# Where VectorE forms the modulation sums in the feed-forward of a three-layer fp32 block chain

## Chip, cores and metric

One core of one Trainium2 chip (trn2) runs the whole program in one launch. The metric is the device time of the launch in microseconds (us); lower is better. All data are fp32 in HBM.

## What is computed

The reference applies two layers of a diffusion-like block (each modulated by vectors made from `c` and `c_ctx`) and then a third block to 256 tokens, beside which run 256 context tokens. Cut to what matters here:

```
mod = silu(c) @ ada_w[l] + ada_b[l]          # six parts of 1024: sh1, sc1, g1, sh2, sc2, g2
h = h + g1 * mixer(rms_norm(h, norm1_g) * (1 + sc1) + sh1)
h = h + g2 * ((silu(a @ w1) * (a @ w3)) @ w2)   with a = rms_norm(h, norm2_g) * (1 + sc2) + sh2
```

The feed-forward of the first layer works on 512 tokens (latent and context), with `w1` and `w3` of 1024 x 2816 and `w2` of 2816 x 1024. While it runs, the kernel also makes the rest of the modulation: `g2` of layer 0 and all six parts of layer 1. `silu(c) @ ada_w` is a product of one or two vectors with a large matrix.

## The kernel before

**Weights.** fp32 products are made on TensorE from two parts of each number. A weight tile of up to 1 MB (128 x 2048) is loaded by SyncE's queue (SP) into `raw` of a slot of SBUF; ScalarE copies it rounded to `whi` (line 1339), VectorE subtracts to get `wlo` over `raw` (line 1840), and TensorE then does three products per block of 128 rows (`mm3`, lines 860 to 862). A slot is free again when the tile's last product is done.

**Modulation sums.** Parts 5 to 11 of the list `MODS` are not made on TensorE. For each there are four tiles of `ada_w`, transposed on the host, of 128 x 2048, and VectorE multiplies each half of such a tile with a row of `silu(c)` or `silu(c_ctx)` and adds up along the row (`summed`, line 1873: a `scalar_tensor_tensor` with `accum_out`). A tile takes four such instructions where both vectors are wanted, two where only one is; at the fourth tile of a part a small `tensor_tensor` adds the bias (line 1893). A sum's tile lies in a slot as a weight tile does, and frees it when its last product is done.

**The order of tiles.** TensorE's program, in a first pass without a chip, lays down the list `TILES`: in the feed-forward, one sum's tile behind each weight tile (`consumed`, line 839, takes the next of `SUMS[12:]`), 28 in all. The document calls the 36 weight tiles of this stage W0 to W35, and the sum's tiles S0 to S27; S0 lies between W0 and W1, S27 between W27 and W28. Tiles take the least recently used of four slots, so as long as the two kinds alternate, the weight tiles go back and forth between the slots named 140/139 and 69/68 (`wlo`/`raw`), and the sum's tiles between 63/60 and 67/64.

The stage has two blocks. Block 1 is W0 to W17, block 2 is W18 to W35. Each has twelve tiles of `w1` and `w3` in turn (`ff1`, `ff3`; two features of 128 per tile, the last two tiles of a block one feature and half the size) and then six of `w2` (`ff2`, two halves of three tiles; the third is of three quarters the size). S0 to S11 take four products each, S12 to S27 two. After W11 a small transpose and a copy hand out the gate row (`gate_rows(5)`).

**Who loads in which order.** SP loads tiles in the order of `loaded()` (line 573): the weight tile first and the sum's tile before it in `TILES` second, so W1, S0, W2, S1 and so on. Each load waits until the slot's previous tile is done, and all later loads wait behind it.

**Who prepares when.** ScalarE and VectorE call `feed(event)` ahead of each step. It goes through the tiles that are new within two tiles of the product named by the event (`next_tiles`, line 583). ScalarE makes the high parts and skips sum's tiles. VectorE's `feed` (line 1831) puts a sum's tile on the list `owed` when it meets it, and makes the low part of a weight tile. Owed sums are formed in two places: before a low part whose own or an earlier load needs the slot that a sum still holds (`held_by`), and at the end of `feed`, if the sum's tile lies before the event's tile. `add(n)` does up to n instructions of the oldest owed sum; `at["sums"]` is 0 up to the end of the first attention (there the sums are spread over its steps) and 4 from there on, set at line 2236.

In the steady state of the feed-forward the order on VectorE is thus: low part of W2, sum S0, activation work of the pair (lines 2264 and 1907: `silu(w1 part) * w3 part`, two features, and their low parts), low part of W3, sum S1, low part of W4, sum S2, activation work, and so on. Each step of TensorE on two features takes one weight tile.

Of the kernel before, what the change touches and what calls it, by code (L numbers as in the profile page):

```python
# [156 lines left out]
class Book:  # L157
# [5 lines left out]
    def did(self, name, *key, by=1):  # L163
        sem = SEM_OF.get(name, name)
        self.now[sem] += by
        if self.counting:
            assert (name, *key) not in self.at, (name, key)
            assert self.by.setdefault(sem, self.engine) == self.engine, (name, sem)
            self.at[name, *key] = sem, self.now[sem]
        assert self.at[name, *key] == (sem, self.now[sem]), (name, key)  # L170
        return self.sems.get(sem), by
# [105 lines left out]
def _build(nc, ctx, I, cst_d, scr_d, out_d, packed):  # L277
# [295 lines left out]
    def loaded():  # L573

        out, held = [], []
        for i, t in enumerate(TILES):
            held.append(i)
            if not t.sums:
                out += held[-1:] + held[:-1]
                held = []  # L580
        return out

    def next_tiles(at, *events):
        n = max([place[event] for event in events], default=0)
        busy = max([i for i in range(max(n - 4, 0), n) if not TILES[i].sums], default=0)
        while at["tile"] < len(TILES):
            i, t = at["tile"], TILES[at["tile"]]
            if t.gate != at["gate"] or t.slot not in at["slots"] or i >= n + at["ahead"] or (not t.sums and t.prev is not None and t.prev >= min(n - 1, busy)):
                return
            at["tile"] += 1  # L590
            yield i, t
# [1225 lines left out]
    def vector_program(e):  # L1817
        at = dict(tile=0, due=Due(book), gate="", chain=0, ahead=2, sums=0, slots={0, 1, 2, *slot_e}, begun=None, owed=[])

        def due(*events):  # L1820
            return at["due"](*events)
# [8 lines left out]
        def feed(*events):  # L1830
            n = max([place[event] for event in events], default=0)
            for i, t in next_tiles(at, *events):
                if t.sums:
                    at["owed"].append(i)
                    continue
                while at["owed"] and held_by(at["owed"][0]) <= loaded().index(i):
                    add(9)
                for s, m in due(("hi", i)):
                    e.wait_ge(s, m)
                e.tensor_tensor(t.lo(), t.raw(), t.hi().bitcast(F32), ALU.subtract).then_inc(*did("lo", i))  # L1840
            while at["sums"] and at["owed"] and at["owed"][0] < n:
                add(at["sums"])

        def held_by(i):

            return next((loaded().index(j) for j in range(i + 1, len(TILES)) if TILES[j].prev == i), len(TILES))

        def add(n):

            i = at["owed"][0]  # L1850
            if at["begun"] is None:
                at["begun"] = summed(i, TILES[i])
            for _ in range(n):
                if next(at["begun"], None) is None:
                    at["begun"] = None
                    at["owed"].pop(0)
                    return
# [5 lines left out]
        def summed(i, t):  # L1863
            p, jj = t.sums
            gate, nv = MODS[p][3], vectors_of(p)
            for s, n in due((f"raw{t.slot}", i), ("cb",), *gm_free(p)):
                e.wait_ge(s, n)
            for c in range(2):
                for v in range(nv):
                    k = 2 * jj + c  # L1870
                    x = GM_OF[p][:, v * 8 + k:v * 8 + k + 1] if gate else MODT_OF[p][:, 2 * k + v:2 * k + v + 1]
                    junk = slot_sum[t.slot][:, (c * nv + v) % 2 * 1024:(c * nv + v) % 2 * 1024 + 1024]
                    m = e.scalar_tensor_tensor(out=junk, in0=slot_raw[t.slot][:, c * 1024:c * 1024 + 1024], scalar=1.0,  # L1873
                                               in1=CB[:, v * D:(v + 1) * D], op0=ALU.mult, op1=ALU.mult, accum_out=x)
                    if (c, v) == (1, nv - 1):
                        m.then_inc(*did("msum", p, jj))
                    elif v == nv - 1:
                        m.then_inc(*link())
                        for s, n in linked():
                            e.wait_ge(s, n)  # L1880
                    yield True
            if jj < 3:
                return
            l, part = MODS[p][:2]
            bias = VT[:, VROW["ada_b"] + l * 48 + part * 8:VROW["ada_b"] + l * 48 + part * 8 + 8]
            for s, n in due(("msum", p, 3)):
                e.wait_ge(s, n)
            if gate:
                x, b3 = v3(GM_OF[p][:, 0:8 * nv], nv), bias.rearrange("p (o k) -> p o k", o=1).broadcast_to([128, nv, 8])
            else:  # L1890
                x = MODT_OF[p].rearrange("p (k v) -> p k v", v=2)[:, :, 0:nv]
                b3 = bias.rearrange("p (k o) -> p k o", o=1).broadcast_to([128, 8, nv])
            e.tensor_tensor(x, x, b3, ALU.add).then_inc(*did("gsum" if gate else "spr", p))

        def gate_rows(p):
            added(p)
            n_ = 8 * MODS[p][3]
            feed(("gt", p))
            for s, n in due(("gt", p), *([("gw", past_gate(p))] if past_gate(p) else [])):
                e.wait_ge(s, n)  # L1900
            e.tensor_copy(G16[0:n_, :], bank("gt", p)[0:n_, 0:128]).then_inc(*did("gcp", p))
            empties(("gt", p), ("gcp", p))
# [23 lines left out]
        def norm_turned(N, p):  # L1926
            w = NORM[N]
            sc, sh, gains = w["mod"][p]
            for k0 in range(0, KT, 2):
                feed(("nt", N, p, k0))  # L1930
                c = p * 4 + k0 // 2
                if k0 % 4 == 0:
                    for s, n in due(("nt", N, p, k0), *gains, *(tm_free(N, c)), *w["tm_free"]):
                        e.wait_ge(s, n)
                    for k in (k0, k0 + 1):
                        o = slice((k - k0) * 256, (k - k0) * 256 + 256)
                        i_ = bank("nt", N, p, k0)[:, o]
                        if sh is None:
                            m = e.tensor_scalar(w["tm"][c % 3][:, o], i_, sc(k), None, ALU.mult)
                        else:  # L1940
                            m = e.tensor_scalar(w["tm"][c % 3][:, o], i_, sc(k), sh(k), ALU.mult, ALU.add)
                    m.then_inc(*did("ntm_v", N, p, k0))
                    empties(("nt", N, p, k0), ("ntm_v", N, p, k0))
                if k0:
                    norm_lo(N, p, k0 - 2)
            norm_lo(N, p, KT - 2)
# [9 lines left out]
        def row(p, hf):  # L1956
            g = 2 * p + hf
            feed(("mod", p, hf, 1))
            for s, n in due(("mod", p, hf, 1), *row_used(p, hf)):
                e.wait_ge(s, n)  # L1960
            e.tensor_copy(GROW[g % 2][0:4, :], bank("mod", p, hf)[0:4, :]).then_inc(*did("grow", p, hf))
            empties(("mod", p, hf), ("grow", p, hf))
# [980 lines left out]
```

## Time and profile before

| | |
|---|---|
| median of 3 runs | 2064.36 us (2060.88 to 2065.09) |
| the profiled execution | 2061.86 us |
| its span in the trace | 2060.0 us |
| TensorE busy | 1789.2 us, 87% |
| VectorE busy | 1246.3 us, 60% |
| ScalarE busy | 823.7 us, 40% |
| mean of DMA traffic | 161 GB/s |
| feed-forward of layer 0 | about 390 to 776 us of the span |

The profiled execution's own time is 1.9 us above its span, which is what lies around the traced part. Rows of the timeline begin with the start in us from the start of the span and the duration in us; an instruction's idle time before it and what ended it stand in square brackets. TensorE's granted clock is given as a share: 1.00 is 2.4 GHz, 0.50 is 1.2 GHz.

### The profile page before, as it was taken

The numbers are of one execution on the slowest core, as the hardware profiler recorded it, in microseconds if no ns is written. First come the engines' busy times: TensorE is split into PE (matmuls) and PEld (weight loads), VectorE is DVE, ScalarE is ACT, GpSimd is POOL, SyncE is SP. The second block draws the span as 40 slices with busy tenths as digits, with TensorE's granted clock in tenths as the row PEclk, the third lists the DMA queues.
The fourth block names the chain that finished last, engine by engine and source line by source line (L and its number), as shares of the span: only waits on it lengthen the run. The fifth ranks groups of instructions, "written<-read, shape, count | busy, mean of one in ns | idle before, by whom it ended". The sixth has DMA issues, their size and how long they took to land. (4 is left out here: it accounts for less than half of the span.)

```text
span 2060.0 us, 21353 instructions
## 1 busy us (share of the span) xinstructions
PE 1789.2 (87%) x8622; PEld 1485.9 (72%) x8622; DVE 1246.3 (60%) x1716; ACT 823.7 (40%) x996; POOL 116.7 (6%) x116
## 2 busy tenths in 40 slices
PE   4988999699799995859767999999987899878997
PEld 2766777487678884749646888888867866668986
DVE  5455782377545535554636888888875555555643
ACT  5222231422113224222314777677744433525532
POOL 1310001000100011320010000000000000000000
PEclk8897988799999997975676999999998999998999
DMA  6322331255545432210033888888855521125552
GB/s 277 102 102 93 132 125 39 102 189 184 194 158 204 163 113 73 84 67 13 1 137 109 326 324 332 324 325 324 322 197 179 176 93 40 62 94 194 183 194 102
DMA packets 61146, 332.54 MB, mean 161 GB/s; under 512 B 16804, under 2 KB 17379, under 8 KB 27890
## 3 DMA queue, kind: packets, MB, share of 16 engines
q1 hardware_dynamic: 55792, 321.54, 42.8%
q10 hardware_dynamic: 4354, 6.32, 0.9%
q0 software_dynamic: 896, 3.26, 0.4%
q8 instruction: 70, 1.15, 0.2%
q14 instruction: 34, 0.27, 0.0%
HBM read 329.96 MB, written 1.13 MB: 161 GB/s over the span
## 5 line engine op out<-in xcount | busy, mean ns | idle before, releaser
L1840 DVE TENSOR_TENSOR wlo__69<-raw__68,whi__70 128x2048 fp32r<-128x2048 f32 (+3 forms) x64 | 136.1, 2127 | 93.4 <-ACT whi__70 L1339 93.4
L1840 DVE TENSOR_TENSOR wlo__65<-raw__64,whi__66 128x2048 fp32r<-128x2048 f32 (+4 forms) x55 | 123.4, 2244 | 76.3 <-ACT whi__66 L1339 76.3
L1840 DVE TENSOR_TENSOR wlo__61<-raw__60,whi__62 128x2048 fp32r<-128x2048 f32 (+4 forms) x56 | 108.6, 1939 | 86.2 <-ACT whi__62 L1339 86.2
L1339 ACT ACTIVATE whi__70<-raw__68 128x2048 fp32r<-128x2048 f32 (+3 forms) x64 | 114.1, 1783 | 115.1 <-DMA raw__68<-in_ffn_w 47.9
L1339 ACT ACTIVATE whi__66<-raw__64 128x2048 fp32r<-128x2048 f32 (+4 forms) x55 | 100.0, 1818 | 77.0 <-DMA raw__64<-in_ev_w_in 21.6
L1339 ACT ACTIVATE whi__62<-raw__60 128x2048 fp32r<-128x2048 f32 (+4 forms) x56 | 91.2, 1628 | 72.8 <-DMA raw__60<-in_ev_w_in 20.7
L2757 POOL TENSOR_TENSOR keep__58<-keep__58,keep__59 128x1 f32<-128x1 f32 (+3 forms) x48 | 45.4, 948 | 1199.3 <-DVE keep__58 L1912 1199.3
L1339 ACT ACTIVATE whi__141<-raw__139 128x2048 fp32r<-128x2048 f32 (+2 forms) x16 | 28.1, 1754 | 126.9 <-DMA raw__139<-in_ffn_w 126.9
L860 PE MATMUL ps<-ffn__120,wlo__140 128*128 128x512 f32 x176 | 70.3, 399 | 9.8 <-DVE wlo__140 L1840 7.0
L1840 DVE TENSOR_TENSOR wlo__140<-raw__139,whi__141 128x2048 fp32r<-128x2048 f32 (+2 forms) x16 | 33.5, 2092 | 72.5 <-ACT whi__141 L1339 72.4
L2095 DVE TENSOR_REDUCE keep__58<-ps 128x1 f32<-128x256 f32 (+1 forms) x104 | 56.6, 544 | 28.5 <-PE ps L862 21.7
L861 PE MATMUL ps<-ffn__121,whi__141 128*128 128x512 f32 x176 | 70.1, 398 | 0.0
L862 PE MATMUL ps<-ffn__120,whi__141 128*128 128x512 f32 x176 | 69.7, 396 | 0.0
L860 PE MATMUL ps<-ffn__120,wlo__69 128*128 128x512 f32 x168 | 65.6, 391 | 2.1 <-issue 2.1
L862 PE MATMUL ps<-ffn__120,whi__70 128*128 128x512 f32 x168 | 65.4, 389 | 0.0
L861 PE MATMUL ps<-ffn__121,whi__70 128*128 128x512 f32 x168 | 65.3, 389 | 0.0
L1873 DVE SCALAR_TENSOR_TENSOR wsum__71<-raw__68,silu_rows 128x1024 f32<-128x1024 f32 x48 | 56.7, 1219 | 2.9 <-DMA raw__68<-in_ada_w 2.8
L1840 DVE TENSOR_TENSOR wlo__218<-raw__217,whi__219 128x2048 fp32r<-128x2048 f32 x24 | 54.9, 2286 | 4.1 <-ACT whi__219 L1339 4.1
L1840 DVE TENSOR_TENSOR wlo__222<-raw__221,whi__223 128x2048 fp32r<-128x2048 f32 x24 | 54.8, 2284 | 0.0
L1840 DVE TENSOR_TENSOR wlo__226<-raw__225,whi__227 128x2048 fp32r<-128x2048 f32 (+1 forms) x24 | 50.6, 2108 | 3.8 <-ACT whi__227 L1339 3.8
L1339 ACT ACTIVATE whi__219<-raw__217 128x2048 fp32r<-128x2048 f32 x24 | 45.8, 1910 | 6.9 <-DMA raw__217<-in_moe_w 6.9
L1873 DVE SCALAR_TENSOR_TENSOR wsum__63<-raw__60,silu_rows 128x1024 f32<-128x1024 f32 x40 | 48.0, 1222 | 0.5
(1069 smaller groups left out, 5376.7 us busy)
## 6 DMA issues: line engine op xcount, KB each, us to landing
raw__217<-in_moe_w SPq DMA_DIRECT2D x24, 1024.0 KB, 6.6
raw__221<-in_moe_w SPq DMA_DIRECT2D x24, 1024.0 KB, 6.7
raw__225<-in_moe_w SPq DMA_DIRECT2D x16, 1024.0 KB, 5.7
raw__68<-in_moe_w SPq DMA_DIRECT2D x16, 1024.0 KB, 6.3
raw__64<-in_moe_w SPq DMA_DIRECT2D x16, 1024.0 KB, 6.8
raw__60<-in_ada_w SPq DMA_DIRECT2D x15, 1024.0 KB, 5.8
raw__64<-in_ada_w SPq DMA_DIRECT2D x15, 1024.0 KB, 5.7
raw__68<-in_ffn_w SPq DMA_DIRECT2D x14, 1024.0 KB, 4.9
```

The source lines that it names most:

```text
L860: e.matmul(out, ll, rh, start=start, stop=False)
L861: e.matmul(out, lh, rl, start=False, stop=False)
L862: return e.matmul(out, lh, rh, start=False, stop=stop)
L1339: e.activation(t.hi(), t.raw(), ACT.Copy).then_inc(*did("hi", i))
L1840: e.tensor_tensor(t.lo(), t.raw(), t.hi().bitcast(F32), ALU.subtract).then_inc(*did("lo", i))
L1873: m = e.scalar_tensor_tensor(out=junk, in0=slot_raw[t.slot][:, c * 1024:c * 1024 + 1024], scalar=1.0, in1=CB[:, v * D:(v + 1) * D], op0=AL ...
L2095: e.tensor_reduce(neg, b[:, 0:u.total], AX.X, ALU.max).then_inc(*link())
L2757: e.tensor_tensor(x, x, EXPO[:, 0:1].broadcast_to([128, n_]) if n_ > 1 else EXPO[:, 0:1], ALU.pow).then_inc(*did(out, *key))
```

## The change

In VectorE's `feed`, when a sum's tile is met and `at["sums"]` is not 0, the sum is formed on the spot, in full, before the low part of the next weight tile. Nothing else is touched: the tiles, their slots, SP's order of loads, ScalarE's and TensorE's programs stay.

```diff
@@ -1832,6 +1832,8 @@
             for i, t in next_tiles(at, *events):
                 if t.sums:
                     at["owed"].append(i)
+                    while at["sums"] and at["owed"]:
+                        add(at["sums"])
                     continue
                 while at["owed"] and held_by(at["owed"][0]) <= loaded().index(i):
                     add(9)
```

With it VectorE's order in the feed-forward is: low part of W0, sum S0, low part of W1, sum S1, low part of W2, activation work, sum S2, low part of W3, sum S3, low part of W4, activation work, and so on. The number of instructions is the same. Outside the feed-forward no sum's tile is met while `at["sums"]` is not 0.

## Rows read from the trace of the kernel before

**Rows 1.** The page's first part: busy us, share of the span, instructions.

```profile
PE 1789.2 (87%) x8622; PEld 1485.9 (72%) x8622; DVE 1246.3 (60%) x1716; ACT 823.7 (40%) x996; POOL 116.7 (6%) x116
```

**Rows 2.** Busy time by stretch: length, PE, PEld, DVE, ACT, POOL, PEclk, DMA, GB/s.

```profile
425.50:447.30 21.80, 21.80 (x98) 17.88 (x96) 16.29 (x23) 5.96 (x6) 0.00 (x0) 1.00 0.56 194
...
625.00:647.00 22.00, 22.00 (x98) 18.22 (x98) 12.09 (x15) 6.26 (x7) 0.00 (x0) 1.00 0.50 193
```

**Rows 3.** Timeline of PE: first products of weight tiles of the feed-forward.

```profile
425.52 0.39 PE L860 MATMUL ps<-ffn__120,wlo__69 128*128 128x512 f32 x1
...
436.40 0.39 PE L860 MATMUL ps<-ffn__120,wlo__140 128*128 128x512 f32 x1
...
508.12 0.47 PE L860 MATMUL ps<-ffn__120,wlo__69 128*128 128x512 f32 x1 [0.75 <-issue]
...
516.55 0.47 PE L860 MATMUL ps<-whi__141,ffn__128 128*128 128x512 f32 x1 [2.60 <-DVE wlo__140 L1840]
...
530.54 0.47 PE L860 MATMUL ps<-whi__70,ffn__128 128*128 128x512 f32 x1 [2.87 <-DVE wlo__69 L1840]
...
557.98 0.79 PE L860 MATMUL ps<-whi__70,ffn__128 128*128 128x512 f32 x1 [6.48 <-DVE ffn__135 L2146]
...
593.13 0.64 PE L860 MATMUL ps<-ffn__120,wlo__140 128*128 128x512 f32 x1 [2.79 <-issue]
...
607.25 0.47 PE L860 MATMUL ps<-ffn__120,wlo__69 128*128 128x512 f32 x1 [1.37 <-issue]
```

**Rows 4.** Timeline of DVE: one pair of block 1, then the end of a two-product sum.

```profile
432.80 2.29 DVE L1840 TENSOR_TENSOR wlo__140<-raw__139,whi__141 128x2048 fp32r<-128x2048 f32 x1 [2.93 <-ACT whi__141 L1339]
435.00 1.22 DVE L1873 SCALAR_TENSOR_TENSOR wsum__63<-raw__60,silu_rows 128x1024 f32<-128x1024 f32 x1
...
439.71 0.68 DVE L2264 TENSOR_TENSOR ffn__134<-ffn__131,ps 128x512 f32<-128x512 f32 x1
...
443.08 0.69 DVE L1907 TENSOR_TENSOR ffn__128<-ffn__132,ffn__127 128x512 fp32r<-128x512 f32 x1 [0.70 <-ACT ffn__127 L1384]
...
451.92 0.17 DVE L1893 TENSOR_TENSOR keep__54<-keep__54,keep__51 128x16 f32<-128x16 f32 x1
...
554.83 1.22 DVE L1873 SCALAR_TENSOR_TENSOR wsum__67<-raw__64,silu_rows 128x1024 f32<-128x1024 f32 x1
...
557.24 0.69 DVE L2146 TENSOR_TENSOR ffn__135<-ps,keep__57 128x512 f32<-128x512 f32 x1
```

**Rows 5.** Timeline of SP: loads of weight tiles (139, 68) and a sum's tile (64).

```profile
403.95 0.33 SPq L2861 DMA_DIRECT2D raw__139<-in_ffn_w  x1
404.32 0.44 SPq L2861 DMA_DIRECT2D raw__64<-in_ada_w  x1
...
425.71 0.33 SPq L2861 DMA_DIRECT2D raw__139<-in_ffn_w  x1
...
595.84 0.43 SPq L2861 DMA_DIRECT2D raw__68<-in_ffn_w  x1
```

**Rows 6.** Issues to landing (last column, us): sum's tiles issued at 404.32, 618.82, 502.33.

```profile
raw__64<-in_ada_w SPq DMA_DIRECT2D x1, 1024.0 KB, 7.0
...
raw__60<-in_ada_w SPq DMA_DIRECT2D x1, 1024.0 KB, 8.3
...
raw__60<-in_ada_w SPq DMA_DIRECT2D x1, 1024.0 KB, 5.8
```

**Rows 7.** Timeline of ACT: the high part of the tile loaded at 425.71.

```profile
430.85 1.92 ACT L1339 ACTIVATE whi__141<-raw__139 128x2048 fp32r<-128x2048 f32 x1 [8.01 <-DMA raw__139<-in_ffn_w]
```

**Rows 8.** Stretches as in rows 2: the wait before W12, then W13, W15, W18.

```profile
514.00:518.00 4.00, 1.45 (x7) 1.24 (x7) 3.88 (x4) 0.56 (x2) 0.00 (x0) 1.00 0.89 352
530.54:543.18 12.64, 12.63 (x49) 10.24 (x49) 1.76 (x1) 1.48 (x1) 0.56 (x1) 0.86 0.47 183
557.98:571.14 13.16, 13.16 (x48) 10.67 (x49) 4.04 (x4) 1.92 (x1) 4.99 (x4) 0.83 0.47 194
593.13:605.72 12.59, 12.59 (x48) 10.05 (x48) 8.08 (x14) 1.92 (x1) 5.05 (x4) 0.86 0.65 251
```

## Prediction

> **What bounds the kernel now.** I read the page first: TensorE is busy 87% of the span [rows 1]. Then the stretches of the one stage where the change acts, the feed-forward. In a pair of weight tiles of block 1 and in one of block 2 TensorE is busy throughout, at the full clock [rows 2]: it bounds the stage, and any time by which a weight tile comes late is lost. VectorE is busy 16.3 of 21.8 us in block 1 and 12.1 of 22.0 in block 2 [rows 2], so it has room, but only over a pair, not at each point of it. Third, TensorE's timeline: a weight tile lasts 10.9 us (425.52 to 436.40), and the idle stretches stand at W11, W12, W13, W15, W18 and W19 [rows 3]. Fourth, how late a weight tile is made ready: its load leaves 0.2 us after the product before it ends (425.71 for 425.52) [rows 3, 5], ScalarE starts 5.1 us later and takes 1.9 [rows 7], the low part runs 432.80 to 435.09 [rows 4], and TensorE wants it at 436.40 [rows 3]. The margin is 1.3 us. The sum that follows the low part at 435.00 is already beyond that point and costs TensorE nothing.
>
> **The change, part by part.** The same instructions run; 28 sums move from behind a low part to in front of one. Two things then stand between a weight tile's load and its product: the wait for the sum's own tile, and the sum.
>
> Terms, in us. (a) The sum's tile is issued 0.37 behind the weight tile [rows 5]: SP's order is as before, and the sum two back, which holds its slot, is now always done. It landed 7.0 after its issue once and 8.3 after it another time [rows 6], so 7.4 to 8.7 behind the weight tile's issue. I take 7.7, nearer the first, because it is the landing inside this steady stretch; the ends stay for the range. Behind a tile of half the size it is 0.4 + 5.8 = 6.2 [rows 6]; behind three quarters I put 6.8, between the two. (b) Four products take 4.7 (435.00 to 439.71), with the bias 0.2 more; two take 2.4 (554.83 to 557.24) [rows 4]. (c) The low part takes 2.2 to VectorE's next instruction (432.80 to 435.00) and 2.4 to TensorE's start: 2.3 of duration, and 0.05 as from line 2146's end (557.93) to 557.98 [rows 3, 4]. Of half size I put 1.2 and 1.3, half of it. (d) The activation work takes 4.1 (439.71 to 443.77) [rows 4].
>
> *W1* (no cost). S0 is loaded ahead of the stage, W1's low part has a whole tile of TensorE as its cover.
>
> *Block 1, the four even tiles W2, W4, W6, W8.* Counted from the first product of the odd tile before: load at 0.2, sum's tile at 7.9, products to 12.6, low part, TensorE starts at 15.0. It wanted to start at 10.9: **+4.1 each**. *The odd tiles between.* Their load leaves at 11.1, their sum's tile lands at 18.8; VectorE has just finished the activation work (14.8 + 4.1 = 18.9). Products to 23.6, TensorE could start at 26.0 and is busy until 25.9: nothing. Four times 4.1 and 0.2 of bias twice: 16.8.
>
> *The clock.* A wait of 2.60 left the granted clock at 1.00; waits of 2.87 and 2.79 were followed by tiles at a mean of 0.86 that lasted 12.6 instead of 10.9, one of 6.48 by 13.2 at 0.83 [rows 3, 8]. So in these rows the wait of 2.60 kept 2.4 GHz, and those of 2.79 and 2.87 were followed by a while at 1.2 GHz that cost 1.7 us. The new waits of 4.1 are longer than both: 4 x 1.7 = 6.8. The even tile then ends at 27.6, and the odd tile's preparation is hidden outright. The Trainium skill (TensorE: Matmul & The Clock Gate, section Why this matters for your kernels) asks for no idle gap above about 3 us between bursts; by it the waits of 2.87 and 2.79 should have been free, and the trace says they were not. By that rule the four waits of 4.1 still cost the clock, and the sum would be the same.
>
> *The end of block 1.* W10 (half size): 0.2 + 6.2 + 4.7 + 1.3 = 12.4 against 10.9: +1.5. W11: its load leaves 1.3 before W10's start, so it starts 6.2 + 4.7 + 1.3 - 1.3 = 10.9 after it; before, 5.4 + 0.9 (the 0.75 of idling and the tail of a product [rows 3]) = 6.3: +4.6. W12: load 5.6 after W10's start, then 7.7 + 4.9 + 2.4, so 9.7 after W11's start; before 8.4 (508.12 to 516.55) [rows 3]: +1.3. W13 was 14.0 behind W12 (to 530.54) because S11 and the low part queued up on VectorE; now only 2.4 of products stands before it, it waits for TensorE alone, at 10.9 or with a slow clock 12.6, I take 11.5: -2.5. W13 itself ran at 0.86 for 12.6 [rows 8]; W14 follows after 0.2 + 6.8 + 2.4 + 1.8 = 11.2: -1.4. W15 waited for line 2146, which stood behind the low part of W15 and two sums; it began 14.8 after W14 (543.18 to 557.98) [rows 3, 8]. Now: load and sum's tile 7.7, products 2.4, low part 2.2, line 2146 0.7, so 13.1: -1.7. W16, nothing; W17 +0.3. W18: 12.4 behind W17 instead of 11.1 (571.14 + 10.9 = 582.02 to 593.13) [rows 3, 8]: +1.3. W19 began 14.1 after W18; its load had been held by SP behind S17's, which waited for S15, until 595.84 [rows 5]. Now that load leaves when W17 is done, the wait of 1.37 [rows 3] goes, and W19 follows at 12.6: -1.5. Together: +1.5 + 4.6 + 1.3 - 2.5 - 1.4 - 1.7 + 0.3 + 1.3 - 1.5 = +1.9.
>
> *Block 2, W20, W22, W24, W26.* 0.2 + 7.7 + 2.4 + 2.4 = 12.7 against 10.9: +1.8 each and 0.2 of bias twice: 7.6. These waits are shorter than the one of 2.60, so no clock. The odd tiles: sum's tile at 11.1 + 7.7 = 18.8, start possible at 23.6, TensorE busy until 12.7 + 10.9 = 23.6: nothing. From W28 on there are no sums.
>
> *Queues.* On SP no load waits longer for a sum than before. POOL's gate row load after W11 shifts with the stage and has the same room before line 2146. ScalarE waits for activation work that comes later, and its next high part is done well before VectorE ends the next sum. The stages behind start from the last residual of this one, so nothing takes the delay up.
>
> Sum: 16.8 + 6.8 + 1.9 + 7.6 = **33 us**. Against the profiled execution, 2061.86, this gives 2095. The median of the runs shown is 2.5 us higher; I keep 2095, 31 above it.
>
> **Rivals.**
>
> *The clock holds.* If the waits, spread differently against the clock's steps, leave it at 1.00, the 6.8 go: 26, so 2088. For it: the wait of 2.60 did so [rows 3, 8]. Against: 4.1 is well over both waits that did not. 15%.
>
> *Late landings.* If the sum's tile lands at 8.7 every time [rows 6], the four even tiles of block 1, the tiles W10 to W12, W15, W18 and the four of block 2 take 1.0 more, 13 in all; block 2's waits become 2.8, as long as the one that cost the clock, 4 x 1.7 more, less what W13's slack takes. That is about 18 more: 2113. In between, half of the landings late, 2104. For it: one of the two rows. Against: the steady stretch showed the early one. 15%.
>
> *Faster: sums fill VectorE's wait.* VectorE idles 2.9 us before the low part of W4 [rows 4], since the weight tile has to land and be rounded. A sum in that gap would be free, if its tile is in SBUF by then; the change also ends the queueing before W13 (2.87 and the 1.7 of clock), W15 (1.7) and W19 (1.37) [rows 3, 8], some 8 us: 2054. It decides at one point: whether the sum's tile lands before VectorE reaches it, that is 5 us or more before what (a) says. SP puts it behind the weight tile, which itself waits for TensorE [rows 5], so this needs a load a tile earlier than the code issues it. 5%.
>
> *No change to speak of.* The sum is met but, by the bounds of `add` or of the two tiles ahead, ends up where it was, or gains and losses cancel: 2062 to 2066. The loop empties the list each time, and the margin of a weight tile is 1.3 against a sum of 4.7. 4%.
>
> **How the numbers follow.** The forecast has 61%, the rivals 39. The range takes in the clock that holds with early landings (33 - 6.8 - 0.3 x 13 = 22, so 2084) and half of the late landings (2104), widened by the 2 us that runs of the kernel lie apart on either side and by the unknown phase of the clock in the later stages: 2081 to 2108. What is outside is most of the last two rivals and half of the late one. A measurement can tell about 0.2%, 4 us, from no change. Slower by more: the forecast, the first two rivals and a bit: 0.91. Within: 0.04. Faster: 0.05.
>
> **What would show it.** In the changed trace: a sum's products stand directly before each low part up to W28's; the idle time of VectorE before line 1873 is ended by the DMA of its raw tile, some 2 to 3 us each time; TensorE waits near 4 us before W2, W4, W6, W8 for `wlo__140`, near 2 in block 2, with 0.86 of clock in the four tiles of block 1 only; the wait of 6.48 before W15 shrinks to about 4.7; pairs of tiles are 27.6 apart in block 1 and 23.6 in block 2, against 21.8; the last product of the stage ends near 809 instead of 776. The forecast is wrong if VectorE starts the sums without waiting for DMA, if the even tiles' waits are gone, or if the stages behind give the time back.

## The result, and the profile after

The change makes the kernel slower: 2097.56 us (2095.81 to 2102.17, four runs) against 2063.70 (2060.88 to 2065.09, four runs) of the kernel before on the same chip, a ratio of 1.0172 [1.0155, 1.0189]. The forecast was 2095, 31 us above the median of before; it is 34. The profiled execution took 2095.81 us.

The page of the changed kernel, its span and first rows [answering to rows 1]:

```profile
span 2094.0 us, 21353 instructions
PE 1797.1 (86%) x8622; PEld 1488.8 (71%) x8622; DVE 1248.8 (60%) x1716; ACT 823.3 (39%) x996; POOL 118.5 (6%) x116
```

No engine has more to do; the span is 34 us longer. The three stages of the changed kernel, cut where the feed-forward's first product and its last one lie. The columns are the stretch, its length, then PE, PEld, DVE, ACT and POOL busy with their instructions, the granted clock, the DMA share and GB/s:

```profile
0.00:388.00 388.00, 313.95 (x1441) 242.74 (x1441) 218.51 (x349) 127.48 (x194) 44.98 (x40) 0.88 0.35 124
388.00:811.00 423.00, 378.76 (x1585) 306.75 (x1585) 214.84 (x264) 90.60 (x82) 19.81 (x15) 0.96 0.41 152
811.00:2094.00 1283.00, 1104.40 (x5596) 939.34 (x5596) 815.45 (x1105) 605.18 (x721) 53.75 (x62) 0.89 0.47 172
```

The same stretches of the kernel before:

```profile
0.00:388.00 388.00, 315.67 (x1441) 244.72 (x1441) 218.35 (x348) 127.51 (x193) 45.05 (x40) 0.87 0.35 124
388.00:776.00 388.00, 368.59 (x1585) 302.24 (x1585) 210.68 (x262) 90.87 (x83) 17.78 (x14) 0.97 0.45 166
776.00:2060.00 1284.00, 1104.92 (x5597) 938.91 (x5596) 817.28 (x1107) 605.27 (x721) 53.86 (x62) 0.89 0.47 172
```

The stage is 35 us longer between these cuts, and those around it are unchanged. PE's busy time grew by 10 us with the same 1585 products: that is mostly the lower clock. The other 25 are idle. Product by product, the stage runs from 390.29 to 809.29 us, 419.00, where it took 385.63 (390.54 to 776.17): +33.4.

PE's timeline of the changed kernel, first products of W2, W3, W4, W6, W15, W18, W19, W20 and W24 (in brackets the idle time before one, and what ended it) [rows 3]:

```profile
418.20 0.47 PE L860 MATMUL ps<-ffn__120,wlo__140 128*128 128x512 f32 x1 [3.62 <-DVE wlo__140 L1842]
...
430.81 0.39 PE L860 MATMUL ps<-ffn__120,wlo__69 128*128 128x512 f32 x1
...
446.87 0.76 PE L860 MATMUL ps<-ffn__120,wlo__140 128*128 128x512 f32 x1 [5.02 <-issue]
...
473.75 0.77 PE L860 MATMUL ps<-ffn__120,wlo__140 128*128 128x512 f32 x1 [3.50 <-issue]
...
582.41 0.50 PE L860 MATMUL ps<-whi__70,ffn__128 128*128 128x512 f32 x1 [4.37 <-DVE ffn__135 L2148]
...
618.50 0.77 PE L860 MATMUL ps<-ffn__120,wlo__140 128*128 128x512 f32 x1 [3.88 <-issue]
...
631.98 0.39 PE L860 MATMUL ps<-ffn__120,wlo__69 128*128 128x512 f32 x1
...
644.75 0.47 PE L860 MATMUL ps<-ffn__120,wlo__140 128*128 128x512 f32 x1 [1.73 <-issue]
...
692.92 0.47 PE L860 MATMUL ps<-ffn__120,wlo__140 128*128 128x512 f32 x1 [2.40 <-issue]
```

Every even tile now has a wait in front of it, no odd tile of the steady stretches has one: 3.62, 5.02, 3.50, and 3.73 before W8 (501.09) in block 1, 1.73, 1.42, 2.40 and 1.52 in block 2 (W22 and W26 at 668.22 and 716.48). Behind a wait in block 1 the tile also lasts longer (430.81 - 418.20 = 12.61, where one took 10.9).

VectorE's timeline over the same pair [rows 4]:

```profile
411.06 1.23 DVE L1875 SCALAR_TENSOR_TENSOR wsum__67<-raw__64,silu_rows 128x1024 f32<-128x1024 f32 x1 [13.96 <-DMA raw__64<-in_ada_w]
...
414.62 1.22 DVE L1875 SCALAR_TENSOR_TENSOR wsum__67<-raw__64,silu_rows 128x1024 f32<-128x1024 f32 x1
415.77 2.29 DVE L1842 TENSOR_TENSOR wlo__140<-raw__139,whi__141 128x2048 fp32r<-128x2048 f32 x1
...
422.10 1.23 DVE L1875 SCALAR_TENSOR_TENSOR wsum__63<-raw__60,silu_rows 128x1024 f32<-128x1024 f32 x1
```

and SP's, whose loads these are [rows 5]:

```profile
403.73 0.33 SPq L2863 DMA_DIRECT2D raw__139<-in_ffn_w  x1
404.10 0.44 SPq L2863 DMA_DIRECT2D raw__64<-in_ada_w  x1
...
414.61 0.33 SPq L2863 DMA_DIRECT2D raw__68<-in_ffn_w  x1
414.98 0.43 SPq L2863 DMA_DIRECT2D raw__60<-in_ada_w  x1
```

Read together: W2's load leaves at 403.73, its sum's tile 0.37 behind it; VectorE has nothing to do until that tile is there (411.06, 7.3 behind the load), then 4.7 of products, then the low part at 415.77; TensorE starts at 418.20. The odd tile W3 was loaded at 414.61, while TensorE was standing still. Its sum begins at 422.10, with no wait, and its low part is ready before TensorE has finished W2.

VectorE's waits over the stage, total, times and longest:

```profile
DVE wsum__67 L1875 <- DMA raw__64<-in_ada_w: 112.7, 14, 14.0
DVE wsum__63 L1875 <- DMA raw__60<-in_ada_w: 33.2, 10, 9.9
```

Before, the weight tiles' high parts ended these waits (72.4 and 58.0 us); now the DMA of the sum's tile ends them.

### The profile page after: what moved, and what is told of

The parts are those of the page before. It is cut to its first block and busy times, and to the rows that moved or that the text cites. A ratio compares the mean times of both kernels' runs of the same rounds, so it can differ in the third digit from the quotient of the medians.

```text
span 2094.0 us, 21353 instructions
## 1 busy us (share of the span) xinstructions
PE 1797.1 (86%) x8622; PEld 1488.8 (71%) x8622; DVE 1248.8 (60%) x1716; ACT 823.3 (39%) x996; POOL 118.5 (6%) x116
## 5 line engine op out<-in xcount | busy, mean ns | idle before, releaser
L1875 DVE SCALAR_TENSOR_TENSOR wsum__67<-raw__64,silu_rows 128x1024 f32<-128x1024 f32 x40 | 49.0, 1248 | 113.2 <-DMA raw__64<-in_ada_w 112.7
L860 PE MATMUL ps<-ffn__120,wlo__140 128*128 128x512 f32 x176 | 74.4, 422 | 35.0 <-issue 24.4
L861 PE MATMUL ps<-ffn__121,whi__141 128*128 128x512 f32 x176 | 72.8, 413 | 0.0
L862 PE MATMUL ps<-ffn__120,whi__141 128*128 128x512 f32 x176 | 72.3, 411 | 0.0
L860 PE MATMUL ps<-ffn__120,wlo__69 128*128 128x512 f32 x168 | 66.6, 396 | 5.2 <-issue 5.2
L1875 DVE SCALAR_TENSOR_TENSOR wsum__63<-raw__60,silu_rows 128x1024 f32<-128x1024 f32 x40 | 49.5, 1261 | 33.8 <-DMA raw__60<-in_ada_w 33.2
L860 PEld LDWEIGHTS ps<-ffn__120,wlo__140 128*128 128x128 f32 x176 | 35.7, 203 | 46.8 <-issue 32.0
L861 PE MATMUL ps<-ffn__121,whi__70 128*128 128x512 f32 x168 | 66.3, 395 | 0.0
L862 PE MATMUL ps<-ffn__120,whi__70 128*128 128x512 f32 x168 | 66.3, 394 | 0.0
L1875 DVE SCALAR_TENSOR_TENSOR wsum__71<-raw__68,silu_rows 128x1024 f32<-128x1024 f32 x48 | 56.7, 1219 | 2.5 <-DMA raw__68<-in_ada_w 2.4
```

What stands on the lines that cost most here:

```text
L860: e.matmul(out, ll, rh, start=start, stop=False)
L861: e.matmul(out, lh, rl, start=False, stop=False)
L862: return e.matmul(out, lh, rh, start=False, stop=stop)
```

## The experiments

Four explanations were open. **In series:** the sum's tile lands some 7.4 us behind the weight tile's load, its products take 4.7, and both stand before the low part. **The wait alone**, whatever stands behind it. **The products alone**, being work in front of the low part. **The loads:** SP's transfers are later or slower. The expectations also name the clock, which takes its part of the cost only if the waits bring it down. Each median below is of four to six runs. The medians of the kernel before beside them were 2061.21 (the first four kernels), 2062.31 (the next four) and 2061.99 (the last two).

**behind.** The list of owed sums is emptied in the same pass of `feed`, but on the other side of the low part:

```diff
                 if t.sums:
                     at["owed"].append(i)
-                    while at["sums"] and at["owed"]:
-                        add(at["sums"])
                     continue
...
                 e.tensor_tensor(t.lo(), t.raw(), t.hi().bitcast(F32), ALU.subtract).then_inc(*did("lo", i))
+                while at["sums"] and at["owed"]:
+                    add(at["sums"])
```

> Each sum is formed as soon as its tile is met, but right behind the low part of the next weight tile instead of in front of it. Theory A (the low part is late because the sum's landing and its products stand in front of it): no low part waits for a sum, SP's loads leave as early as with the change, so the waits before W2 to W8 are gone and those before W13, W15 and W19 shrink: 2056 (2050 to 2061), 8 below the kernel before. Rival B (the sum's load right behind the weight tile's takes bandwidth from it, whatever VectorE does): the loads still leave together, so it stays near 2095.

Measured: 2051.79 us, ratio 0.9952 [0.9935, 0.9969], so faster than the kernel before. VectorE's timeline at W4:

```profile
433.40 2.29 DVE L1840 TENSOR_TENSOR wlo__140<-raw__139,whi__141 128x2048 fp32r<-128x2048 f32 x1 [3.21 <-ACT whi__141 L1339]
435.61 1.22 DVE L1875 SCALAR_TENSOR_TENSOR wsum__67<-raw__64,silu_rows 128x1024 f32<-128x1024 f32 x1
```

The low part waits for its high part only, as in rows 4, and the sum follows 2.2 us later. Each sum comes about one low part later than in the change (at 413.31 and 425.40 for 411.06 and 422.10). What is left of waits is 0.33 before W5, 0.62 (W11), 2.90 (W12), 4.02 (W15) and 1.36 (W18); those before W13 and W19, for sums that had piled up on VectorE, are gone. So making the sums early isn't what costs, but the side of the low part on which they stand: 46 us lie between the medians of this kernel and the changed one.

**wait_front.** As behind, and where the sum's tile is met VectorE waits for its landing, with no product there:

```diff
                     at["owed"].append(i)
-                    while at["sums"] and at["owed"]:
-                        add(at["sums"])
+                    for s, m in due((f"raw{t.slot}", i)) if at["sums"] else ():
+                        e.wait_ge(s, m)
                     continue
```

> As in the run before it, but VectorE waits for the sum's raw tile in front of the low part and forms the sum behind it. Theory A: the sum's tile lands 7.3 to 7.5 us after the weight tile's load leaves, the high part is there at 7.1, so the low part is 0.4 us later and the margin of 1.3 us covers it: within 2 us of the run before it, 2056. Rival C (the empty wait of VectorE for the DMA is what costs, not the products that follow it): the even tiles are 4 us late as with the change, 2090 or more.

Measured: 2055.18, ratio 0.9962 [0.9946, 0.9977]; 3.4 above behind by the medians, though the two intervals overlap. The wait is real, and in VectorE's waits over the stage it is now the largest:

```profile
DVE wlo__140 L1842 <- DMA raw__64<-in_ada_w: 67.7, 14, 13.3
```

It moves the low part of W4 from 433.40 to 435.15:

```profile
435.15 2.29 DVE L1842 TENSOR_TENSOR wlo__140<-raw__139,whi__141 128x2048 fp32r<-128x2048 f32 x1 [3.81 <-DMA raw__64<-in_ada_w]
```

TensorE stands 0.1 to 1.1 us before a few tiles in the steady stretches (W3, W5, W9, W21) and 2.14 before W11 (0.62 in behind). With the load at 0.2, the landing 7.4 behind it and 2.4 for the low part, the tile is ready some 10 after TensorE took the one before, inside the 10.9. **The wait alone** is refuted: of the 46 us it brings at most these 3.

**load_first.** The changed kernel, but for the feed-forward's sums SP loads a sum's tile ahead of the weight tile that it stands before:

```diff
-                out += held[-1:] + held[:-1]
+                late = [j for j in held[:-1] if TILES[j].sums[0] >= 5]
+                out += late + held[-1:] + [j for j in held[:-1] if j not in late]
```

> VectorE's order as with the change; SP loads the sum's tile ahead of the next weight tile, for the parts 5 to 11. Theory A: the sum's tile leaves as soon as the previous weight tile's load has left, lands a tile's length before it is met, and the sum fits into VectorE's wait for the next weight tile: no wait of TensorE for a low part in the pairs, 2054 (2048 to 2061). Rival D (four products in front of the low part are too long wherever the tile is): the even tiles stay late by 2 us or more, above 2075.

Measured: 2045.27 (2039.87 to 2047.95), ratio 0.9911 [0.9894, 0.9928]. The direction was right; the time is below the range of 2048 to 2061 that was given. VectorE's timeline:

```profile
445.07 2.29 DVE L1843 TENSOR_TENSOR wlo__69<-raw__68,whi__70 128x2048 fp32r<-128x2048 f32 x1
447.28 1.22 DVE L1876 SCALAR_TENSOR_TENSOR wsum__67<-raw__64,silu_rows 128x1024 f32<-128x1024 f32 x1
...
454.64 2.29 DVE L1843 TENSOR_TENSOR wlo__140<-raw__139,whi__141 128x2048 fp32r<-128x2048 f32 x1 [2.58 <-ACT whi__141 L1340]
```

The order on VectorE is that of the change: products, then low part. But the sum's tile is loaded before TensorE lets go of the weight tile's slot, so its products run at 447.28, ahead of the weight tile's landing, in time that VectorE spent idle before. The low part waits for its high part again, as in rows 4. The stage's row:

```profile
388.00:761.00 373.00, 363.43 (x1585) 299.06 (x1585) 216.59 (x262) 91.20 (x82) 21.78 (x14) 0.99 0.45 169
```

The last product ends at 760.25, 16 us before that of the kernel before and 7.0 before that of behind; waits are left before W11 (2.68), W12 (1.33), W15 (1.55) and W18 (1.06), and none within the pairs. **The products alone** is refuted: the same products in front of the same low parts, in the fastest kernel of all.

**filled.** The changed kernel, and on TensorE, ahead of W2, W4, W6 and W8, sixteen more products whose result nothing uses, to see what the waits are worth without the clock:

```diff
         def feat(key, x, src, f0, m, ntok, ready, ring):
+            if key[0] == "ff1" and key[1] == 0 and key[2] in (2, 4, 6, 8):
+                b = take("m", "fill", *key)
+                for c in range(16):
+                    k = c % KT
+                    e.matmul(b, AT4f[0][:, k, 0:128], AT4f[0][:, k, :], start=c == 0, stop=c == 15)
```

> The changed kernel with 16 products of 512 columns (3.6 us) into an unused bank in front of W2, W4, W6 and W8, where TensorE would idle for 3.5 to 5.0 us. Their result is not used. If the clock's fall after those waits is worth 1.6 us each, the four tiles last 10.9 again and the time is 6 below the changed kernel: 2091. If the fall does not come from the idling, the tiles stay at 12.5 and the time is that of the changed kernel, 2097.

Measured: 2092.19 (2088.61 to 2095.64), ratio 1.0137 [1.0115, 1.0159], by the medians 5 to 6 below the two measurements of the changed kernel. That is near the spread of the runs; what decides is the length of the four tiles in the trace. The stretches of W2 and W6 (W4 and W8 read the same):

```profile
417.46:428.47 11.01, 11.01 (x48) 9.06 (x49) 9.31 (x13) 3.56 (x4) 0.00 (x0) 1.00 0.27 113
...
470.84:481.82 10.98, 10.98 (x49) 9.03 (x50) 9.35 (x13) 3.56 (x4) 0.00 (x0) 1.00 0.13 54
```

The same stretches in the changed kernel, for W6, W18 and W24:

```profile
473.75:486.32 12.57, 12.57 (x49) 10.27 (x49) 9.45 (x13) 3.56 (x4) 0.00 (x0) 0.87 0.26 108
...
618.50:631.98 13.48, 13.48 (x49) 10.90 (x49) 8.49 (x9) 1.91 (x1) 6.00 (x4) 0.80 0.21 87
...
692.92:703.92 11.00, 11.00 (x49) 9.08 (x49) 7.14 (x9) 3.56 (x4) 0.00 (x0) 1.00 0.38 162
```

With the waits filled, all four run at 2.4 GHz and take 11.0 instead of 12.3 to 12.6: 6 us over four tiles is the clock's part. The stretch from W0's start to W9's got only 3.9 shorter (119.43 against 123.32), because in this trace the sum's tile landed later twice. SP's timeline, the load of W6's sum's tile:

```profile
455.12 0.43 SPq L2868 DMA_DIRECT2D raw__64<-in_ada_w  x1
```

and VectorE's, its first product:

```profile
463.74 1.23 DVE L1880 SCALAR_TENSOR_TENSOR wsum__67<-raw__64,silu_rows 128x1024 f32<-128x1024 f32 x1 [9.26 <-DMA raw__64<-in_ada_w]
```

8.6 from issue to use, where W2's in the changed kernel took 7.0, and W6 started 16.3 behind W5. That is the rival of late landings, seen on two tiles (8.6 before W6, 8.3 before W8): what the landing is late goes straight on to TensorE.

**block1** and **block2.** The change for the sums S0 to S11 alone, and for those from S12 on alone:

```diff
-                    while at["sums"] and at["owed"]:
+                    while at["sums"] and at["owed"] and t.sums[0] < 8:
```

(block2 has `>= 8`.)

> The change for the sums of four products alone (S0 to S11), the others as before. Theory A: the waits before W2, W4, W6, W8, W10 and W11, the clock after them, and W12: some 29 above the kernel before, less what W13 gives back; block 2 as before: +26 (22 to 31), so 2088. If the effect were one of a few places and not one that adds up tile by tile, it would be all of 36 or near nothing.

> The change for the sums of two products alone (S12 to S27), the ff2 part of block 1 and block 2. Theory A: +1.4 to 1.8 at each of W20, W22, W24, W26, little net in the ff2 part: +6 (2 to 9), so 2068.

Measured: block1 2086.37, ratio 1.0116 [1.0101, 1.0132], +24.1; block2 2070.48, ratio 1.0043 [1.0029, 1.0057], +8.2. They add up to 32.2, against 33.9 and 36.6 for the whole in its two measurements: the cost arises tile by tile. Four products cost more than two: in block 1 of the changed kernel 4.0 a wait on average and the clock, in block 2 waits of 1.4 to 2.4 and a clock that stayed at 1.00.

**load_first_only.** The loads of load_first under the VectorE order of the kernel before, to see what the loads do by themselves. The expectation was reckoned as the forecast was: a held load, then its landing.

```diff
-                out += held[-1:] + held[:-1]
+                late = [j for j in held[:-1] if TILES[j].sums[0] >= 5]
+                out += late + held[-1:] + [j for j in held[:-1] if j not in late]
```

> VectorE's order as in the kernel before, SP's order of loads alone changed as in load_first (sum's tile first). The load of the sum's tile waits for the sum two back, which VectorE forms behind a later low part; the next weight tile's load now queues behind it. Theory A: in the pairs the sum two back is formed 3.5 us after W's load should leave (439.7 against 436.6), so the weight tile is 3 us late with a margin of 1.3 or less: slower than before, 2070 to 2090. If SP's order alone explained the gain of load_first, it would be near 2046.

Measured: 2151.12 (2148.68 to 2153.35), ratio 1.0430 [1.0416, 1.0444]. Slower, as expected, but by 89 us, not 8 to 28. SP's timeline in this kernel, over two tiles:

```profile
452.34 0.33 SPq L2862 DMA_DIRECT2D raw__60<-in_ada_w  x1
452.72 0.43 SPq L2862 DMA_DIRECT2D raw__68<-in_ffn_w  x1
469.36 0.33 SPq L2862 DMA_DIRECT2D raw__64<-in_ada_w  x1
469.73 0.43 SPq L2862 DMA_DIRECT2D raw__139<-in_ffn_w  x1
```

VectorE's timeline over the same tiles:

```profile
445.32 2.29 DVE L1841 TENSOR_TENSOR wlo__140<-raw__139,whi__141 128x2048 fp32r<-128x2048 f32 x1 [10.00 <-ACT whi__141 L1340]
447.53 1.22 DVE L1874 SCALAR_TENSOR_TENSOR wsum__63<-raw__60,silu_rows 128x1024 f32<-128x1024 f32 x1
...
462.34 2.29 DVE L1841 TENSOR_TENSOR wlo__69<-raw__68,whi__70 128x2048 fp32r<-128x2048 f32 x1 [6.05 <-ACT whi__70 L1340]
```

TensorE's, the first products of both:

```profile
447.71 0.77 PE L861 MATMUL ps<-ffn__120,wlo__140 128*128 128x512 f32 x1 [2.98 <-issue]
...
464.73 0.76 PE L861 MATMUL ps<-ffn__120,wlo__69 128*128 128x512 f32 x1 [3.01 <-issue]
```

It is a loop: low part (445.32), the sum behind it (447.53), whose end at 452.3 frees the slot for the next sum's tile (452.34), behind which alone the next weight tile may leave (452.72); that one lands, is rounded, and the low part comes at 462.34. Once around takes 17.0, and TensorE follows (447.71 to 464.73) instead of 10.9. I had priced one held load per tile and not seen that each delay feeds the next load's.

**behind_load_first.** Both at once: the sum straight behind the low part (the diff of behind), the loads of load_first.

> SP's order as in load_first, each sum behind the next low part instead of in front. The sum then frees its slot a tile later than in load_first, and SP's next sum's tile, and the weight tile behind it, wait for that by 1 to 3 us. Theory A: between load_first and the kernel before, 2050 (2044 to 2062). If it makes no difference where the sum stands once it is formed promptly, 2046.

Measured: 2052.01 (2050.09 to 2053.62), ratio 0.9947 [0.9933, 0.9960], the same as behind. One step of the expectation failed: in the pairs of block 1 SP holds the sum's tiles 2.7 to 4.2 us for their slots (one leaves at 418.90, where it would have left at 416.2), but they are out before the next weight tile's slot is free, and that load leaves on time (426.69, W3 having begun at 426.49). With prompt sums the load order costs nothing; it gains only with the products in front. So load_first's advantage is neither the loads alone nor the promptness alone (behind). It arises at the end of block 1: from W11's first product to W19's load_first took 81.2 us and behind 89.5, while in the pairs both run without waits to speak of. There the products run before the low part, in time that VectorE spends waiting for the weight tile; in behind a sum of 2.4 us stands between the low part before W15 (548.11) and line 2148 (552.74), on which W15 waits.

**half_products.** The changed kernel with each product of S0 to S11 taken over 512 of its 1024 columns, which leaves out half of each of these sums:

```diff
+                    w_ = 512 if 5 <= p < 8 else 1024
+                    junk = slot_sum[t.slot][:, (c * nv + v) % 2 * 1024:(c * nv + v) % 2 * 1024 + w_]
+                    m = e.scalar_tensor_tensor(out=junk, in0=slot_raw[t.slot][:, c * 1024:c * 1024 + w_], scalar=1.0,
+                                               in1=CB[:, v * D:v * D + w_], op0=ALU.mult, op1=ALU.mult, accum_out=x)
```

> The changed kernel with the products of S0 to S11 over 512 of 1024 columns, so half of each of these sums is left out. A sum then takes some 2.5 us instead of 4.7, everything else stays. Theory A (the sum's length in front of the low part passes to TensorE one for one, and shorter waits keep the clock): the waits before W2, W4, W6, W8 fall from 3.5 to 5.0 by 2.2 each to about 1.6, no slow clock behind them (4 x 1.6), 2.2 less before W11 and about 1 before W10 and W12: 20 us below the changed kernel, 2077 (2072 to 2083). Rival C (what costs is the empty wait for the DMA): 2097 as the changed kernel.

Measured: 2086.71 (2085.98 to 2089.90), ratio 1.0120 [1.0104, 1.0135]: 12 below the changed kernel measured beside it (changed_again, below), not the 20 expected. The first product before W4's low part, in VectorE's timeline:

```profile
435.08 0.69 DVE L1876 SCALAR_TENSOR_TENSOR wsum__67<-raw__64,silu_rows 128x512 f32<-128x512 f32 x1 [8.38 <-DMA raw__64<-in_ada_w]
```

0.69 each, four of them 2.7 with what lies between: 2.0 less than 4.7 (2.2 reckoned), and the waits before W2, W4, W6 and W8 fell to 1.46, 2.25, 1.44 and 0.35. Up to W9 the stage gained 12.8 us on changed_again (111.4 against 124.2 from W0's start to W9's) where 15.2 had been expected; the rest of the 20 was to come at the end of block 1, and there it gained 0.8 (117.7 against 118.5 from W9's start to W19's). Two things took some of it back before W9. Waits of 1.05 and 2.23 appeared before W7 and W9, whose sums' tiles landed 8.3 and 8.4 us after their issue; behind those of W3 and W5, at 7.0, TensorE did not wait. And the clock fell over W4 and W9. TensorE's timeline at W4 and W9:

```profile
440.25 0.47 PE L860 MATMUL ps<-ffn__120,wlo__140 128*128 128x512 f32 x1 [2.25 <-issue]
...
502.44 0.47 PE L860 MATMUL ps<-ffn__120,wlo__69 128*128 128x512 f32 x1 [2.23 <-issue]
```

and the stretches that begin there:

```profile
440.25:452.86 12.61, 12.61 (x49) 10.22 (x49) 7.31 (x13) 3.55 (x4) 0.00 (x0) 0.86 0.35 148
502.44:515.05 12.61, 12.61 (x49) 10.26 (x49) 5.06 (x11) 2.66 (x4) 0.00 (x0) 0.86 0.26 107
```

So the size of the products is a term of the cost, and no more than one: shorter ones shrink it, and what waits next comes up. Why the end of block 1 gained so little no run took apart; W11 still waited 4.61, and W13 and W15 1.76 and 4.53.

**changed_again.** The changed kernel once more, beside half_products.

> The changed kernel once more, on the chip and in the call of the run before it, so that the two are compared directly: 1.017 times the kernel before, about 2097.

Measured: 2098.61 (2092.83 to 2099.65), ratio 1.0171 [1.0157, 1.0186].

**The loads** as the cause are refuted by behind, which issues the two loads 0.4 us apart as the change does and is faster than the kernel before. The changed kernel's trace agrees: each weight tile lands 4.7 to 5.1 us after its issue in the steady stretches, as before (6.1 and 6.0 the two times, W4 and W24, that its sum's tile took 7.8 and 8.1), and no load is held longer than before; W19's leaves at 614.66, as soon as W17 is done, where a sum had held it.

## Why the prediction was right, point by point

The mechanism and the size were right. By its own steps (W0 to W9 cost 23.0 for 23.6 forecast, W9 to W19 2.0 for 1.9, W19 to W27 8.3 for 7.6):

- *Even tiles of block 1, +4.1 each and 0.4 of bias, 16.8.* The waits are 3.62, 5.02, 3.50 and 3.73, together 15.9. In block 1 the sum's tile landed 7.2 to 7.5 behind the weight tile's load, not 7.7, and 8.5 behind it once (weight tile issued at 431.00, sum's tile at 431.76 and landed 7.8 later), which is W4's 5.02. wait_front, load_first and half_products show that it takes both the landing and the products.
- *The clock, 4 x 1.7 = 6.8.* The tiles lasted 12.61, 12.34, 12.57 and 12.52: 6.5 in all. W0 to W9 took 123.3; the steps gave 123.9 (100.3 before, and 16.8 and 6.8). Shown by filled, whose four tiles ran at 1.00.
- *The end of block 1, +1.9.* W10's wait was 1.20 (1.5 predicted); W11 began 10.84 behind W10 (10.9), W12 9.72 behind W11 (9.7), W13 12.18 behind W12 (11.5), W14 11.01 (11.2), W15 12.81 (13.1) with a wait of 4.37 (4.7), W16 12.60 behind W15 where I had said unchanged at 13.2, W17 11.21 (11.2), W18 12.28 (12.4). The sum came out by luck in part: W13 was 0.7 later than reckoned, since it did not wait for TensorE alone (its sum's tile landed 8.3 after its issue, and TensorE stood 1.06), and W19 0.9 later, 13.48 behind W18 for 12.6, as over W18, after the wait of 3.88, the clock was at 0.80 of full and not at 0.86; W16's 0.6 and smaller differences took that back.
- *Block 2, 7.6.* From W19 to W27 95.5 us, against 87.2 before: 8.3. The waits are 1.4 to 2.4, where 1.8 was reckoned: the 2.40 before W24 is again a sum's tile that landed late (8.5 behind the weight tile's load, the others 7.4 to 7.7). The clock is at 1.00 over all four tiles (W20, W22, W24, W26). That it would be, because the waits are shorter than 2.60, was luck for W24: waits of 2.23, 2.25 and 2.38 in other kernels brought it down (last section).
- *The odd tiles, nothing.* None has a wait in the steady stretches. The cover is thin: in the kernels with the change's order, where a sum's tile took 8.3 to 8.4 us before an odd tile, TensorE waited (0.91 before W27 in changed_again; 1.05, 2.23 and 1.11 before W7, W9 and W27 in half_products; 1.21 and 2.38 before W23 and W25 in filled).
- *The stages behind take nothing up.* 1283.0 against 1284.0. The last product stood at 809.29; "near 809" was forecast.

Of the rivals, *the clock holds* would have taken off 6 us, as filled's tiles show. *Late landings* came now and then, not every time: in the changed kernel three sums' tiles (before W4, W13 and W24) took 7.8, 8.3 and 8.1 us from their own issue, the others behind a weight tile of full size 6.8 to 7.6; in filled four took 8.3 to 8.6 and one 10.2. *Faster, sums fill VectorE's wait* named its own point: whether the sum's tile has landed before VectorE reaches it. In the changed kernel it has not. In load_first it has, and the kernel comes to 2045, below the 2054 I gave it: I counted W13, W15 (1.7) and W19, but there the wait before W12 also falls from 2.60 to 1.33, and that before W15 from 6.48 to 1.55.

One detail was wrong. VectorE's idle time before a sum was to be "some 2 to 3 us each time". It is 9 to 14 in front of the even tiles of block 1 (13.96 in the row at 411.06) and nothing in front of the odd ones (422.10), in block 2 8 to 11 and 1.3 to 2.5: VectorE has run out of work long before the load leaves, and the wait is counted from there. The 2 to 3 us were the part behind the weight tile's landing. It changed no term of the sum. The base was a little off too: 33 us added to the profiled 2061.86, and the runs' median was 2063.7, to which 33.9 came.

What stays open is what decides on the clock between waits of 2.0 and 3.5 us (below); no run took it apart.

## What to carry to other kernels

Work that has room on its engine over a period can still cost its full length if it stands, with its own wait for data, in front of what the bottleneck waits for; put it behind, or load its data a slot earlier, so that it fills the wait rather than follows it (here 2098, 2052 and 2045 us for the same instructions). Look at the order in which a queue loads together with the order in which an engine uses: here either half alone cost 34 and 89 us, and both together gained 16. The work put behind, with the loads as before, gained 10. When a load that is held holds others, look for a loop before you price it once.

## What the runs showed of the hardware

- Of two 1 MB loads issued 0.4 us apart by SP, in the changed kernel the first landed 4.7 to 5.1 us after its issue (6.0 and 6.1 twice), the second 6.8 to 7.6 (7.8 to 8.3 three times); the latest was 10.2 in filled, while the first took 8.1. The sum's tiles that the kernel before issued in the pairs up to W8, 2.9 to 4.4 us behind the weight tile (417.80 to 473.41), landed in 4.7 to 4.9.
- The granted clock doesn't follow the length of the wait alone. In the kernel before, a wait of 2.60 kept it at 1.00, in the changed one 2.40 (W24, above), in block2 3.52 (W18). Waits of 2.23 (twice) and 2.25 in half_products, one of 2.38 in filled (W25) and one of 1.95 in wait_front (W12, behind a tile of half size that had itself waited 2.14) were followed by tiles at 0.86 to 0.87. The stretch of W25 in filled:

```profile
700.46:713.09 12.63, 12.63 (x49) 10.25 (x49) 5.96 (x7) 3.52 (x4) 0.00 (x0) 0.86 0.34 141
```

  PE's timeline at W18 in block2, and the stretch that begins there:

```profile
597.03 0.47 PE L860 MATMUL ps<-ffn__120,wlo__140 128*128 128x512 f32 x1 [3.52 <-issue]
...
597.03:608.03 11.00, 11.00 (x49) 9.09 (x49) 8.36 (x9) 1.92 (x1) 6.04 (x4) 1.00 0.28 118
```

  The Trainium skill (TensorE: Matmul & The Clock Gate, section Why this matters for your kernels) asks for no idle gap above about 3 us. These traces agree for the waits before W2, W4, W6 and W8 of the changed kernel (3.50 to 5.02, each with a slower tile behind it), but a wait of 3.52 kept the full clock once, and slower tiles followed shorter waits too: two of them in the kernel before (2.79 and 2.87) [rows 3, 8]. A tile of full size lasted 12.3 to 12.8 us in these cases, where at 1.00 it takes 10.9 to 11.1.
- A product of 128x1024 with its sum took 1.22 us on VectorE, one of 128x512 0.69.
